# Six more weight chunks held in ring slots, queries of a head pair in two pieces

## The reference, cut to what matters

```python
def peer_ffn(h, w_q, sub_keys, u, v):              # h: [256, 1024]
    q = (h @ w_q).reshape(T, 8, 2, 128)            # w_q: 1024 x 2048
    s1, s2 = q[:, :, 0] @ sub_keys[0].T, q[:, :, 1] @ sub_keys[1].T
    # top 16 of each, top 16 of the 256 sums: 8 heads x 16 = 128 experts a token
    hb = einsum('td,tkd->tk', h, u[ids])
    act = gelu(hb) * gate
    return einsum('tk,tkd->td', act, v[ids])
x = x + attention_retention_mixer(rms_norm(x), ...)   # layer 0, ends in @ w_o
x = x + peer_ffn(rms_norm(x), ...)
x = x + conformer_conv_module(rms_norm(x), ...)       # layer 1: @ w1, GLU, 31 taps, norm, @ w2
x = x + peer_ffn(rms_norm(x), ...)
return rms_norm(x)
```

## Time and profile before

| | us |
|---|---|
| median of 3 runs (lowest, highest) | 1573.75 (1571.93, 1573.99) |
| the profiled execution | 1575.5 |
| its span, first to last instruction | 1573.8 |
| PE busy, matmuls (share of the span) | 1069.3 (68%) |
| VectorE busy | 1100.9 (70%) |
| ScalarE busy | 514.8 (33%) |
| POOL busy | 691.9 (44%) |
| data moved | 615.95 MB, mean 391 GB/s |

### The profile page before, as it was taken

How to read it: one execution, slowest core, us unless ns; L and a number is a source line. 1 busy time by engine, 2 the same in 40 slices (tenths; PEclk the granted TensorE clock), 3 DMA queues, 4 the chain that set the end, 5 groups by cost and what they waited for, 6 DMA issues and landing times.

```text
span 1573.8 us, 20663 instructions
## 1 busy us (share of the span) xinstructions
PE 1069.3 (68%) x6966; PEld 532.1 (34%) x6966; DVE 1100.9 (70%) x2839; ACT 514.8 (33%) x1569; POOL 691.9 (44%) x566
## 2 busy tenths in 40 slices
PE   7999857677656476666666678656776657555655
PEld 7796433333313143322333345312433313111111
DVE  2745577778878578986457889899548877744555
ACT  3222314333322344424323444424333233322223
POOL 0002434444434266675343445575334344545552
PEclk9999978887878689788778889958887778777687
DMA  9146899999999999999999999999999999999996
GB/s 381 60 142 272 352 421 421 420 420 421 421 414 421 420 393 415 417 391 421 421 421 421 421 419 408 421 397 411 421 421 421 421 421 420 415 414 421 421 421 274
DMA packets 86027, 615.95 MB, mean 391 GB/s; under 512 B 9504, under 2 KB 10272, under 8 KB 12704
## 3 DMA queue, kind: packets, MB, share of 16 engines
q0 software_dynamic: 73728, 536.90, 82.7%
q1 hardware_dynamic: 12048, 77.45, 12.2%
q10 hardware_dynamic: 144, 0.26, 0.0%
HBM read 613.53 MB, written 1.05 MB: 391 GB/s over the span
## 4 chain that ended last, share of the span: by engine, by line
DMA 65%; DVE 15%; PE 13%; ACT 2%; issue 2%; DVEq 1%; POOL 1%; ACTq 0%; SPq 0%; POOLq 0%
DMA ring<-experts_dram,idx_now 65%; DVE ring L1016 6%; PE pm L1213 6%; DVE conv_buf L1085 5%; PE side L1465 3%; PE side L1213 2%; ACT L648 1%; POOL ring L472 1%; ACT diag_all L637 0%; DMA x_tok<-x_dram 0%; DVE top_i L936 0%; PE side L1436 0%; PE pm L1354 0%; DVE onehot L937 0%; ACT act_v L631 0%
## 5 line engine op out<-in xcount | busy, mean ns | idle before, releaser
L472 POOL DMA_INDIRECT ring<-experts_dram,idx_now x512 | 676.3, 1321 | 735.0 <-DMA ring<-experts_dram,idx_now 465.4
L1465 PE MATMUL side<-ring,diag_all 64*64 64x512 f32 x2056 | 663.2, 786 | 474.6 <-ACT diag_all L637 467.3
L1016 DVE SCALAR_TENSOR_TENSOR ring<-ring,h_tok 128x1024 f32<-128x1024 f32 x512 | 611.0, 1224 | 246.6 <-DMA ring<-experts_dram,idx_now 239.8
L1465 PE MATMUL pm<-ring,diag_all 64*64 64x512 f32 x2040 | 659.5, 788 | 0.0
L1465 PEld LDWEIGHTS side<-ring,diag_all 64*64 64x64 f32 x2056 | 156.3, 164 | 914.7 <-ACT diag_all L637 652.0
L628 ACT ACTIVATE ge<-hb 128x2 f32<-128x2 f32 (+1 forms) x257 | 52.4, 204 | 805.1 <-DVE ring L1016 794.3
L637 ACT ACTIVATE diag_all<-ident,act_v 128x64 f32<-128x64 f32 x512 | 150.6, 341 | 21.3 <-issue 0.4
L1465 PEld LDWEIGHTS pm<-ring,diag_all 64*64 64x64 f32 x2040 | 155.3, 165 | 0.0
L631 ACT ACTIVATE act_v<-ge,gates 128x1 f32<-128x1 f32 x512 | 123.4, 287 | 17.7
L1085 DVE SCALAR_TENSOR_TENSOR conv_buf<-conv_buf,chan_sb 128x128 f32<-128x128 f32 x480 | 129.0, 350 | 0.0
L1213 PEld LDWEIGHTS side<-h_t,wbuf 128*128 128x128 f32 x640 | 73.5, 194 | 10.6 <-issue 10.6
(11 more groups left out here) (205 smaller groups left out, 939.9 us busy)
## 6 DMA issues: line engine op xcount, KB each, us to landing
wbuf<-wq_dram SPq DMA_DIRECT2D x24, 1024.0 KB
wbuf<-w_dram SPq DMA_DIRECT2D x16, 1024.0 KB
ring<-w_in_dram SPq DMA_DIRECT2D x5, 2048.0 KB, 22.9
wbuf<-w_o_dram SPq DMA_DIRECT2D x8, 1024.0 KB
ring<-experts_dram,idx_now POOLq DMA_INDIRECT x512
ring<-w_dram SPq DMA_DIRECT2D x4, 1024.0 KB, 15.3
gain<-gains_dram SPq DMA_DIRECT2D x7, 512.0 KB, 15.5
ring<-wq_dram SPq DMA_DIRECT2D x2, 1024.0 KB, 9.9
```

Of the source, the lines that this page charges most:

```text
L472: pool.indirect_dma_start(ring[:, r, :], None, table[layer], bass.IndirectOffsetOnAxis(idx_now[:, i % 2, n - n0:n - n0 + 1], 0)) \
L1016: dve.scalar_tensor_tensor(out=ring[:, slot, 0:D], in0=ring[:, slot, 0:D], scalar=1.0, in1=h_tok[:, t, :], op0=ALU.mult, op1=ALU.mult, acc ...
L1465: step = pe.matmul(acc[odd][c][j * HALF:(j + 1) * HALF, :], diag[rows, r % (2 * BATCH), :], ring[rows, slot, D + c * COLS:D + (c + 1) * COLS],
```

## The change

Three things change. (1) A list KEPT names twelve chunks that are loaded into ring slots, against six before; AWAY says from which pick and to which pick a slot is taken from the picks. New in it are the query chunks 2 and 3 of layer 0 (slots 14, 15, from pick 14 on), w1 chunks 4 and 5 (slots 10, 11, from pick 128 on) and layer 1's query chunks 4 and 5 (slots 8, 9, from pick 224 on); w1 0 and 1 go to slots 14 and 15, w1 2 and 3 to 12 and 13, layer 1's query chunks 6 and 7 to 14 and 15. Slots 10 to 13 come back at pick 312, 8 and 9 at 404, 14 and 15 at 424. The picks have 16 slots to pick 13, 14 to 127, 10 to 223, 8 to 311, 12 to 403, 14 to 423, then 16. (2) SyncE's order follows: the second tile's first two w_o chunks stand ahead of the kept query chunks 2 and 3; a kept load waits for the last use of the chunk held before it in its slot, or for the slot's last pick, or for `b_t_ready`. (3) PE multiplies the queries of a head pair at b = 2 and b = 3, one head each, instead of both at b = 3, and `heads_start` stands one place earlier; the `both_queries(p, 3)` at (1, 0) of phases 2 and 3 stays.

```diff
-KEPT = 4
-KEPT_IN = {("w1", c): RING - KEPT + c for c in range(KEPT)} | {("q", 6): RING - KEPT, ("q", 7): RING - KEPT + 1}
-KEPT_FROM = PICKS
-KEPT_TO = {RING - KEPT + c: 3 * PICKS + 2 * RING if c < 2 else 2 * PICKS + 2 * RING + 8 for c in range(KEPT)}
+KEPT = [("q", 0, 2, 14), ("q", 0, 3, 15), ("w1", 0, 0, 14), ("w1", 0, 1, 15), ("w1", 0, 2, 12), ("w1", 0, 3, 13),
+        ("w1", 0, 4, 10), ("w1", 0, 5, 11), ("q", 2, 4, 8), ("q", 2, 5, 9), ("q", 2, 6, 14), ("q", 2, 7, 15)]
+KEPT_IN = {(kind, p, c): r for kind, p, c, r in KEPT}
+AWAY = {8: (PICKS + 6 * RING, 3 * PICKS + RING + 4), 9: (PICKS + 6 * RING, 3 * PICKS + RING + 4), 10: (PICKS, 2 * PICKS + 2 * RING + 24), 11: (PICKS, 2 * PICKS + 2 * RING + 24), 12: (PICKS, 2 * PICKS + 2 * RING + 24), 13: (PICKS, 2 * PICKS + 2 * RING + 24), 14: (RING - 2, 3 * PICKS + 2 * RING + 8), 15: (RING - 2, 3 * PICKS + 2 * RING + 8)}
...
+def kept_as(kind, p, c):
+
+    of = {"w1": 0, "q": p // 2 * 2}.get(kind)
+    return (kind, of, c) if (kind, of, c) in KEPT_IN else None
...
-    order = [("o", 0, c) for c in range(4)] + [("q", 0, h) for h in range(4)]
-    order += [("o", 1, c) for c in range(4)] + [("q", 0, h) for h in range(4, 8)] + [("q", 1, h) for h in range(4)]
+    order = [("o", 0, c) for c in range(4)] + [("q", 0, 0), ("q", 0, 1)]
+    order += [("o", 1, c) for c in range(4)] + [("q", 0, h) for h in range(4, 8)] + [("q", 1, 0), ("q", 1, 1)]
     for p in (1, 2):
-        order += [("w1", p - 1, c) for c in range(KEPT, KD)] + [("w2", p - 1, c) for c in range(4)]
+        order += [("w1", p - 1, c) for c in range(KD)] + [("w2", p - 1, c) for c in range(4)]
         order += [("q", p + 1, h) for h in range(6)]
-    return order
+    return [chunk for chunk in order if not kept_as(*chunk)]
...
-        free = [r for r in range(RING) if r not in KEPT_TO or not KEPT_FROM <= n < KEPT_TO[r]]
+        free = [r for r in range(RING) if r not in AWAY or not AWAY[r][0] <= n < AWAY[r][1]]
...
             def load_kept(kind, p, c):
 
-                r = KEPT_IN[(kind, c)]
-                if kind == "w1":
-                    sp.wait_ge(v_multiplied, RING + max(n for n in range(KEPT_FROM) if SLOTS[n][0] == r) + 1)
+                r, n = KEPT_IN[(kind, p, c)], KEPT.index((kind, p, c, KEPT_IN[(kind, p, c)]))
+                held = [k for k in KEPT[:n] if k[3] == r]
+                if held:
+                    sp.wait_ge(*last_use(*held[-1][:3]))
+                elif AWAY[r][0] < RING:
+                    sp.wait_ge(b_t_ready, 2)
                 else:
-                    sp.wait_ge(pw_ps, KD + r - RING + KEPT + 1)
+                    sp.wait_ge(v_multiplied, RING + max(n for n in range(AWAY[r][0]) if SLOTS[n][0] == r) + 1)
...
             load_chunks("o", 0, 2, 4)
-            load_chunks("q", 0, 0, 4)
-            load_chunks("o", 1, 0, 4)
+            load_chunks("q", 0, 0, 2)
+            load_chunks("o", 1, 0, 2)
+            for c in (2, 3):
+                load_kept("q", 0, c)
+            load_chunks("o", 1, 2, 4)
             load_chunks("q", 0, 4, 8)
             load_gain("norm", 4)
-            load_chunks("q", 1, 0, 4)
+            load_chunks("q", 1, 0, 2)
             load_gain("bias", 0)
-            for c in range(KEPT):
+            for c in range(6):
                 load_kept("w1", 0, c)
-            load_chunks("w1", 0, KEPT, KD)
+            load_chunks("w1", 0, 6, KD)
             load_gain("norm", 5)
             load_chunks("w2", 0, 0, 4)
             load_chunks("q", 2, 0, 2)
             load_gain("norm", 6)
-            load_chunks("q", 2, 2, 6)
+            load_chunks("q", 2, 2, 4)
+            for c in (4, 5):
+                load_kept("q", 2, c)
             load_gain("bias", 1)
             for c in (6, 7):
                 load_kept("q", 2, c)
-            load_chunks("w1", 1, KEPT, KD)
+            load_chunks("w1", 1, 6, KD)
             load_gain("norm", 7)
             load_chunks("w2", 1, 0, 4)
             load_chunks("q", 3, 0, 2)
             load_gain("norm", 8)
-            load_chunks("q", 3, 2, 6)
+            load_chunks("q", 3, 2, 4)
...
-                if (i, b) == (2, 3):
+                if (i, b) == (2, 2):
                     heads_start(1)
-                if 1 <= i < 7 and b == 3:
-                    both_queries(*SELECTIONS[i + 1])
+                if 1 <= i < 7 and b >= 2:
+                    queries(*SELECTIONS[i + 1], b - 2)
...
-                    if (i, b) == (5, 3):
+                    if (i, b) == (5, 2):
                         heads_start(p + 1)
-                    if i >= 5 and b == 3:
-                        both_queries(p + 1, i - 5)
+                    if i >= 5 and b >= 2:
+                        queries(p + 1, i - 5, b - 2)
```

More of the change, by code:

```diff
@@ L57, with kept_use @@
 X_OF_NORM = [0, 0, 1, 2, 3, 4, 5, 6, 7, 8]
-KEPT = 4
-KEPT_IN = {("w1", c): RING - KEPT + c for c in range(KEPT)} | {("q", 6): RING - KEPT, ("q", 7): RING - KEPT + 1}
-KEPT_FROM = PICKS
-KEPT_TO = {RING - KEPT + c: 3 * PICKS + 2 * RING if c < 2 else 2 * PICKS + 2 * RING + 8 for c in range(KEPT)}
+KEPT = [("q", 0, 2, 14), ("q", 0, 3, 15), ("w1", 0, 0, 14), ("w1", 0, 1, 15), ("w1", 0, 2, 12), ("w1", 0, 3, 13),
[5 more added lines that the diff above has]
+    return (kind, of, c) if (kind, of, c) in KEPT_IN else None
+def kept_use(key):
+    r = KEPT_IN[key]
+    return 16 * ([k[:3] for k in KEPT if k[3] == r].index(key) + 1)
 def weight_chunks():
-    order = [("o", 0, c) for c in range(4)] + [("q", 0, h) for h in range(4)]
-    order += [("o", 1, c) for c in range(4)] + [("q", 0, h) for h in range(4, 8)] + [("q", 1, h) for h in range(4)]
+    order = [("o", 0, c) for c in range(4)] + [("q", 0, 0), ("q", 0, 1)]
+    order += [("o", 1, c) for c in range(4)] + [("q", 0, h) for h in range(4, 8)] + [("q", 1, 0), ("q", 1, 1)]
     for p in (1, 2):
-        order += [("w1", p - 1, c) for c in range(KEPT, KD)] + [("w2", p - 1, c) for c in range(4)]
+        order += [("w1", p - 1, c) for c in range(KD)] + [("w2", p - 1, c) for c in range(4)]
         order += [("q", p + 1, h) for h in range(6)]
-    return order
+    return [chunk for chunk in order if not kept_as(*chunk)]
 CHUNKS = weight_chunks()
@@ L280, in hybrid_decoder_trunk_kernel @@
         gathered = [sem(f"gathered{r}") for r in range(RING)]
-        kept_loaded = [sem(f"kept_loaded{c}") for c in range(KEPT)]
+        kept_loaded = {r: sem(f"kept_loaded{r}") for r in AWAY}
         idx_copied, may_gather = sem("idx_copied"), sem("may_gather")
@@ L360, in multiplied, with last_use @@
                 return (wo_ps if kind == "o" else w2_ps), p * 4 + c + 1
+            def last_use(kind, p, c):
+                if kind == "w1":
+                    return pw_ps, KD + c + 1
+                return q_ps, nth_head(p + 1, c // 2, c % 2)
             def load_kept(kind, p, c):
-                r = KEPT_IN[(kind, c)]
-                if kind == "w1":
-                    sp.wait_ge(v_multiplied, RING + max(n for n in range(KEPT_FROM) if SLOTS[n][0] == r) + 1)
+                r, n = KEPT_IN[(kind, p, c)], KEPT.index((kind, p, c, KEPT_IN[(kind, p, c)]))
[4 more added lines that the diff above has]
+                    sp.wait_ge(b_t_ready, 2)
                 else:
-                    sp.wait_ge(pw_ps, KD + r - RING + KEPT + 1)
+                    sp.wait_ge(v_multiplied, RING + max(n for n in range(AWAY[r][0]) if SLOTS[n][0] == r) + 1)
                 view = {"q": wq_l[p // 2], "w1": w1}[kind]
-                sp.dma_start(ring[:, r, :], view[:, c, :]).then_inc(kept_loaded[r - RING + KEPT], 16)
+                sp.dma_start(ring[:, r, :], view[:, c, :]).then_inc(kept_loaded[r], 16)
             def load_chunks(kind, p, first, end):
@@ L465, in gathers @@
                                 pool.wait_ge(b_t_ready, 2)
-                        if r >= RING - KEPT and n >= KEPT_TO[r] and all(SLOTS[m][0] != r for m in range(KEPT_TO[r], n)):
-                            c = r - RING + KEPT
-                            pool.wait_ge(*((q_ps, nth_head(3, 3, c)) if c < 2 else (pw_ps, KD + c + 1)))
+                        if r in AWAY and n >= AWAY[r][1] and all(SLOTS[m][0] != r for m in range(AWAY[r][1], n)):
+                            kind, of, c = [k[:3] for k in KEPT if k[3] == r][-1]
+                            pool.wait_ge(*((pw_ps, KD + c + 1) if kind == "w1" else (q_ps, nth_head(of + 1, c // 2, c % 2))))
                         if n >= AHEAD:
@@ L1366, in chunk @@
             def chunk(kind, p, c):
[L1368 to L1371, removed]
+                key = kept_as(kind, p, c)
+                if key:
+                    pe.wait_ge(kept_loaded[KEPT_IN[key]], kept_use(key))
+                    return ring[:, KEPT_IN[key], :].rearrange("p (k c) -> p k c", k=KD)
                 n = CHUNKS.index((kind, p, c))
```

## The result

The changed kernel is slower: 1584.99 us (median of 6 runs, 1580.8 to 1586.16) against 1573.87 (6 runs), a ratio of 1.0072, 95% interval 1.0059 to 1.0085. That is +11.1 us where -3.7 was forecast, outside the range that ended at 1580. The profiled execution took 1585.57 us, span 1583.8.

A forecast was written before the change was run, and what follows sets the result against it. The prediction saw two close limits: DMA, mostly expert gathers, and VectorE in the convolution stretches. Its terms -4.0 + 2.5 + 2.8 - 5.0 gave -3.7: 1571.8 us profiled, 1570.0 as a median, range 1561 to 1580.

The forecast's parts named there:

- Eight slots, picks 224 to 311: Waiting for pick n-8 instead of n-12 is mostly free; two tight places, pick 284 at +2.8 and pick 248 at 0.
- I take 7.0: Time assumed from a gather's issue to its dot at the tight places, in us, with about half as many gathers in flight.
- By 560 us the bytes are the same: 0 [...] I take back 4.0: Phase 0: q 2, 3 saved but w1 0, 1 come early, 0; two loads missing in 560 to 700 us, -4.0.
- q 4, 5 moved to 790 us: Layer 1's q 4, 5 loaded early, where VectorE waits for gathers: +2.5, nothing given back at their old place.
- q 4, 5 of the last phase: Two loads fall out of the queue starting at 1161.56, in a stretch at 420 GB/s: -5.0.
- w1 4, 5 of the second tile: Two loads fall out of the queue starting at 937.30, inside VectorE's stretch of 810 to 1070 us: 0.
- The prelude: Second tile's w_o 0, 1 load first, q 2, 3 later into slots 14, 15; early bytes stay the same: 0.
- ten slots: Picks 14 to 223 with 14, then 10 slots; POOL mostly waits for gathers, not slots: 0, or +5 if cover goes.
- the split under cover: Queries in two pieces, away from pick 240: hidden under DMA's cover, 0; a misplaced head costs 3.8 if cover goes.
- a wait for a slot in picks 128 to 223: Named beforehand as one of the signs that the forecast is wrong; no size given.
- Rival B: Slower: eight slots are a bubble in every ring turn, slots return late in phases 1 and 2; 1578.7, chance 0.21.
- Rivals A and C: A: most of the gross saving comes in, 1560, chance 0.18. C: no change, 1572.5, chance 0.16.

The follow-up runs named there:

- e3: The kernel before with only ring slots withheld from the picks (ten, then eight left), no load or product moved: 1587.99 us, ratio 1.0102.
- g3: The kernel before with only slots 10 and 11 withheld from picks 128 to 311, nothing kept in them: 1574.38 us, ratio 1.0003.
- g2: The changed kernel with the second tile's w1 6, 7 loads held back to their old place near 980 us: 1580.31 us, ratio 1.0037.
- e1: The changed kernel with w1 4, 5 not kept, slots 10 and 11 back to the picks, two weight loads more: 1566.8 us, ratio 0.9965.
- f5: The changed kernel with the first tile's w1 6, 7 loads held back to their old place, about 603 us: 1578.71 us, ratio 1.0042.
- f3: The kernel before with only the queries of a head pair split in two pieces: 1573.62 us, ratio 1.0001.
- e2: The changed kernel with layer 1's q 4, 5 not kept, loaded twice at their old places; w1 4, 5 stay kept: 1570.82 us, ratio 0.9986.
- f2: e1 with slots 8 and 9 taken from the picks at pick 236 instead of 224, so q 4, 5 load later: 1567.24 us, ratio 0.9961.
- h1: The changed kernel with w1 6, 7 held back to their old places for both tiles: 1574.73 us, ratio 1.0006.
- g1: The changed kernel with w1 2 to 5 not kept and layer 1's q 4, 5 in slots 12 and 13: 1569.64 us, ratio 0.9966.
- e4: The changed kernel with both heads' queries in one block at b = 3 again: 1581.46 us, ratio 1.0064.
- f1: e1 with both heads' queries in one block at b = 3 again: 1566.07 us, ratio 0.996.

## Why the prediction was wrong

**The step that failed most is "Eight slots, picks 224 to 311": "I take 7.0", and two places, picks 248 and 284.** It gave +2.8 and 0. Eight slots alone cost 14.7 us (e3) and ten cost nothing (g3). At pick 248 the 7.0 was fair. Kernel after, the issue that waits for the slot, and its dot:

```profile
853.40 1.39 POOL L498 DMA_INDIRECT ring<-experts_dram,idx_now  x1 [2.99 <-PE pm L1491]
```

```profile
852.76 1.22 DVE L1042 SCALAR_TENSOR_TENSOR ring<-ring,h_tok 128x1024 f32<-128x1024 f32 x1 [2.00 <-DMA ring<-experts_dram,idx_now]
...
855.76 1.23 DVE L1042 SCALAR_TENSOR_TENSOR ring<-ring,h_tok 128x1024 f32<-128x1024 f32 x1 [1.76 <-DMA ring<-experts_dram,idx_now]
...
859.36 1.24 DVE L1042 SCALAR_TENSOR_TENSOR ring<-ring,h_tok 128x1024 f32<-128x1024 f32 x1 [2.37 <-DMA ring<-experts_dram,idx_now]
...
862.86 0.94 DVE L959 MAX8 top_v<-side 128x8 f32<-128x128 f32 x4 [2.25 <-PE side L1462]
...
866.19 1.22 DVE L1042 SCALAR_TENSOR_TENSOR ring<-ring,h_tok 128x1024 f32<-128x1024 f32 x1
```

853.40 to 859.36 is 6.0. The issue came 1.0 us after the earlier trace rows's 852.40, although the forecast had let it come 3.6 sooner by the split. In the rows are picks 246, 247, 248, each late. The second place came four picks sooner than the forecast's 284, at pick 280, and there the size was off by far:

```profile
943.94 0.97 POOL L498 DMA_INDIRECT ring<-experts_dram,idx_now  x1 [3.86 <-PE pm L1491]
```

```profile
954.24 1.23 DVE L1042 SCALAR_TENSOR_TENSOR ring<-ring,h_tok 128x1024 f32<-128x1024 f32 x1 [1.28 <-DMA ring<-experts_dram,idx_now]
...
959.21 1.23 DVE L1042 SCALAR_TENSOR_TENSOR ring<-ring,h_tok 128x1024 f32<-128x1024 f32 x1 [3.74 <-DMA ring<-experts_dram,idx_now]
```

15.3 us from issue to dot, above the forecast's own upper end of 11.6. That end was read where only gathers were in flight; here four weight loads are issued in the 14 us ahead of it:

```profile
930.11 10.84 SPq L391 DMA_DIRECT2D ring<-wq_dram  x2
941.00 0.91 SPq L402 DMA_DIRECT2D wbuf<-w_dram  x2
```

Before, four loads came in the same place, two of them those of the earlier trace rows's 937.30 and the other two these:

```profile
924.48 12.78 SPq L370 DMA_DIRECT2D ring<-wq_dram  x2
```

They were hidden by landed picks in store: from 905 to 1010 us VectorE waited for no gather. Eight slots had spent that store. Taking two of the four loads away (g2) takes 4.7 us off, and e1, with ten slots and all four loads there, loses nothing from pick 264 to 288 (-1.2): loads and slots cost this together. The second fault lies in the same step: it took the moments at which slots come free from the trace of before. A late dot makes a late product, and that a late slot for the pick eight places on: pick 240's dot, at 837.10 before, came at 840.49, behind the two loads at 790 us, and the slot for pick 248 hangs on it. That lateness grows over several turns of the ring is not shown: in e3 picks 249 to 278 are all 4.0 to 5.3 us late, while their gathers are issued up to 17 us later than before. g3's rows show how much waiting is free: POOL may wait for slots, so long as VectorE has landed picks.

**"By 560 us the bytes are the same: 0 [...] I take back 4.0"**: the 0 held (pick 144 at 558.63 us before, +0.6 after), the 4.0 failed too. Up to pick 224 the kernel after gained nothing beyond what executions differ by; the rate in 560 to 700 fell to 388, where the forecast had it rise; and with the two loads back there the kernel is 4.7 to 6.3 us faster (f5). The 4.1 us that VectorE waited for gathers there was not to be had from these loads: all of it lies ahead of them. Its last row, kernel before:

```profile
571.02 1.23 DVE L1016 SCALAR_TENSOR_TENSOR ring<-ring,h_tok 128x1024 f32<-128x1024 f32 x1 [0.21 <-DMA ring<-experts_dram,idx_now]
```

The loads of w1 6, 7 are issued from 607.53 us on, and from 575 to 700 VectorE waits for no gather. With the loads gone it still waits 5.4 us for gathers in 560 to 700, and POOL, with ten slots, waits for one for 36.7 us in 560 to 784, against 5.3 before:

```profile
DVE ring L1042 <- DMA ring<-experts_dram,idx_now: 5.4, 6, 1.3
...
POOL ring L498 <- PE pm L1491: 36.7, 19, 4.0
```

So the loads there were nearly free, and in front of it they cost about their full price. The 5.0 saved by q 2, 3 was real (f5), and was spent on them.

**q 4, 5 moved to 790 us:** +2.5 was forecast, with nothing back at the old place. In e1 the move costs 6.3 us from pick 224 to 232 and gives 4.6 back up to 264, +1.7 in all: the sum was near, both parts were wrong. What gives it back is not shown; f3, which has the split alone, gains 1.7 over the same picks.

**q 4, 5 of the last phase:** -5.0 forecast. From pick 288 to 424 most kernels that leave them out gain about as much (after, e1, f2, f5, g2, h1: 3.4 to 3.6), but g1 gains 1.0, e4 0.6 and f1 6.0; of those that load them e3 and g3 lose 0.8, f3 loses 2.3, and e2, which leaves out the second load of w1 4, 5 in their place, gains 5.2. The sign fits the forecast; the size, and that it is this pair of loads, is not shown.

**w1 4, 5 of the second tile:** 0 forecast. e1, which loads them, loses nothing against the kernel before from pick 264 to 312 (-5.5, -6.6). Right there; e2's gain says that leaving them out may pay later.

**The prelude, ten slots, the split under cover:** costed at 0. PE waits 0.8 us for q 2 in the kernel after; ten slots and the split alone measure 1.0003 and 1.0001. Right, though "a wait for a slot in picks 128 to 223", named as a sign of being wrong, came (those 36.7 us): VectorE was the limit there, and the wait cost nothing that shows.

The sum, by the column of the kernel after: -1.6 up to pick 224, +6.9 to 264 (1.7 of it the q pair, by e1), +7.4 to 288, -3.4 to 424: +9.3, and +11.1 between the medians. The slots and the loads that meet them are +12.6 of it. (The parts do not simply add: e3, with slots taken and nothing moved, has +7.3 and +5.9 at these places by itself.)

**Rival B was what came,** larger than its 1578.7, and by its mechanism, with a chance of 0.21. Its condition, over 9 us from issue to dot, held at pick 280 (15.3) and not at pick 248 (6.0). The Trainium skill, Perfetto Trace Analysis, § Identifying Performance Opportunities, says that a gap which repeats on the engine that should be saturated can mean too little SBUF for the next tile. e3 agrees with that: with nothing but the slots changed, POOL waits for one 26 times, against 9, and VectorE's waits for gathers go from 16.2 to 34.1 us. The Trainium skill, DMA: Bandwidth & Descriptors, § Anatomy of one DMA, fits 2.0 us plus the bytes at 436 GB/s, by which 1 MB alone takes 4.4 us (an estimate by that page). The 6.0 at pick 248 holds the start of VectorE too, and no run here shows a gather alone there. Rivals A and C fall: VectorE's waits for gathers in 784 to 1060 us rose by 19.2 us, over the 10 that the prediction had named as the mark of B.

## What to carry to other kernels

A buffer that is taken from a ring is not paid for by the idle time it has on average: follow one turn of the ring with the new count, with every release that the turn itself delays, and look for the place where the store of landed data is smallest and other transfers come at once. A load saved, or moved, is worth its time where the transfers are the limit: before moving one, ask which engine limits the stretch it leaves and the one it enters, and whether the waits that it is to remove lie behind it or ahead of it. And make the keeping cheap first: the pair of chunks whose second load cost nothing where it stood (w1 4, 5, with ten slots) is the one not to keep.

## What was not expected of the hardware

From issue to dot a 1 MB gather took 6.0 us with few others in flight, 11.6 with five, and 15.3 beside four weight loads. And one slot pair was worth nothing from twelve to ten (1.0003) and about 14 us from ten to eight (1.0102).
